# A two-block transformer kernel: first weights and tokens loaded in smaller pieces, and one sum of the second feed-forward made ahead of its gate

## What is computed

```python
def first_block(x, ...):
    h = x + mixer_block(rmsnorm(x, norm_mix_gain), w_in, ...)
    h = h + square(relu(rmsnorm(h, norm_mlp_gain) @ w_ff1)) @ w_ff2
    return rmsnorm(h, norm_final_gain)

def second_block(x, ...):
    ...
    u = rms_norm(h, pre_ffn_gain)
    gate_up = u @ w_ffn_in                       # 1024 -> 2 x 2816
    f = (silu(gate_up[..., :D_FF_2]) * gate_up[..., D_FF_2:]) @ w_ffn_out
    return h + rms_norm(f, post_ffn_gain)
```

## Time and profile before

| | |
|---|---|
| median of 3 runs | 929.07 us (928.72 to 931.43) |
| the profiled execution | 927.26 us; its span 925.5 us |
| granted TensorE clock, mean over the span | 0.999 of full |
| TensorE busy | 906.6 us, 98% of the span |
| VectorE busy | 629.2 us, 68% |
| ScalarE busy | 454.7 us, 49% |
| moved by DMA | 148.91 MB, mean 161 GB/s |

### The profile page before, as it was taken

How to read it: one execution, slowest core, us unless ns; L and a number is a source line. 1 busy time by engine, 2 the same in 40 slices (tenths; PEclk the granted TensorE clock), 3 DMA queues, 4 the chain that set the end, 5 groups by cost and what they waited for, 6 DMA issues and landing times.

```text
span 925.5 us, 13962 instructions
## 1 busy us (share of the span) xinstructions
PE 906.6 (98%) x5276; PEld 771.6 (83%) x5276; DVE 629.2 (68%) x1022; ACT 454.7 (49%) x764; POOL 43.5 (5%) x81
## 2 busy tenths in 40 slices
PE   8999999999999999989999999999999999999997
PEld 5888999998888888867776788888999778888885
DVE  5867676666876666676763777777766776666665
ACT  5646534444644444445334555666644644444443
POOL 0000010000100000010000000023310100000000
PEclk9999999999999999999999999999999999999999
DMA  9853333554655555323333222332355255555531
GB/s 347 304 203 137 137 138 137 184 181 163 224 191 194 197 193 181 136 91 137 137 136 137 91 92 92 97 132 92 105 221 206 107 187 207 196 182 181 181 136 46
DMA packets 21921, 148.91 MB, mean 161 GB/s; under 512 B 2400, under 2 KB 3168, under 8 KB 4336
## 3 DMA queue, kind: packets, MB, share of 16 engines
q1 hardware_dynamic: 20704, 145.29, 44.6%
q10 hardware_dynamic: 1168, 2.95, 0.9%
HBM read 147.18 MB, written 1.05 MB: 160 GB/s over the span
## 4 chain that ended last, share of the span: by engine, by line
PE 92%; DVE 3%; ACT 2%; issue 1%; DMA 1%; POOL 0%; SPq 0%; DVEq 0%; ACTq 0%; POOLq 0%
PE ps L432 20%; PE ps L433 19%; PE ps L434 19%; PE ps L547 14%; PE ps L548 7%; PE ps L1421 2%; PE ps L1375 1%; DVE wlo L1511 1%; PE ps L1393 1%; ACT whi L606 1%; PE ps L441 1%; PE ps L1380 1%; PE ps L444 1%; DMA raw<-weights 1%; PE ps L1111 1%
## 5 line engine op out<-in xcount | busy, mean ns | idle before, releaser
L1511 DVE TENSOR_TENSOR wlo<-raw,whi 128x2048 fp32r<-128x2048 f32 x134 | 306.8, 2290 | 152.4 <-ACT whi L606 152.0
L606 ACT ACTIVATE whi<-raw 128x2048 fp32r<-128x2048 f32 x134 | 256.3, 1914 | 184.6 <-PE ps L434 107.3
L547 PE MATMUL ps<-xT,whi 128*128 128x512 f32 x608 | 213.9, 396 | 2.6 <-DVE u_sum L2116 1.9
L548 PE MATMUL ps<-xT,wlo 128*128 128x256 f32 x608 | 169.9, 279 | 0.0
L547 PEld LDWEIGHTS ps<-xT,whi 128*128 128x128 f32 x608 | 114.1, 188 | 30.0 <-DVE wlo L1511 2.2
L432 PE MATMUL ps<-whi,xT 128*128 128x512 f32 (+1 forms) x336 | 133.3, 397 | 3.6 <-DVE wlo L1772 1.9
L434 PE MATMUL ps<-whi,xT 128*128 128x512 f32 (+1 forms) x336 | 129.6, 386 | 0.0
L433 PE MATMUL ps<-wlo,xT 128*128 128x512 f32 (+1 forms) x336 | 129.4, 385 | 0.0
L548 PEld LDWEIGHTS ps<-xT,wlo 128*128 128x128 f32 x608 | 114.6, 189 | 0.7
L432 PEld LDWEIGHTS ps<-whi,xT 128*128 128x128 f32 x336 | 63.1, 188 | 21.8 <-issue 4.3
L432 PE MATMUL ps<-xT,whi 128*128 128x256 f32 x256 | 74.7, 292 | 0.0
(11 more groups left out here) (328 smaller groups left out, 1458.2 us busy)
## 6 DMA issues: line engine op xcount, KB each, us to landing
raw<-weights SPq DMA_DIRECT2D x135, 1024.0 KB, 4.8
cst<-consts SPq DMA_DIRECT2D x1, 1595.0 KB, 13.4
raw<-weights SPq DMA_DIRECT2D x2, 512.0 KB, 6.6
gain_rows<-gain_rows ACTq DMA_DIRECT2D x1, 1024.0 KB, 8.1
y<-h ACTq DMA_DIRECT2D x4, 256.0 KB, 2.3
h<-x_tiles SPq DMA_DIRECT2D x1, 512.0 KB, 7.9
gain_row<-gain_rows ACTq DMA_DIRECT2D x1, 512.0 KB, 3.8
h<-x_tiles ACTq DMA_DIRECT2D x1, 256.0 KB, 3.0
```

The lines of the kernel that those rows point to most:

```text
L547: pe.matmul(ps[:, bank0 + j, :], vh[:, k, j * P:(j + 1) * P], xT[:, :, k, :], start=k == 0, stop=False)
L548: m = pe.matmul(ps[:, bank0 + j, 0:TOK], vl[:, k, j * P:(j + 1) * P], xT_h[:, k, :], start=False, stop=k == KC - 1)
L606: act.activation(whi[s][:], raw[s][:], ACT.Copy).then_inc(split_hi, 1)
L1511: dve.tensor_tensor(wlo[s][:], raw[s][:], whi[s][:], ALU.subtract).then_inc(split_lo, 1)
```

## The change

At the start, blobs 0 and 1 come in five loads, listed in `FIRST` as (blob, first chunk, end chunk), and the tokens in four loads of 256 columns. They are issued in the order of use. ScalarE's and VectorE's conversions and TensorE's multiplications go by the same five parts. The two squares move: the first between the last parts, the second behind the last part. TensorE's warming matmuls after the first pair of transposes are now two of 512 columns, and the second pair of transposes stands behind the first part's matmuls. In the second feed-forward the function `up_product` is split in two, `up_sum` and `up_product`. In the loop and in the last step the order of the instructions stays what it was; in step 1 ScalarE's `up_low` now stands ahead of `gate_sigmoid` and VectorE's sum ahead of `gate_product`, and `up_product` ahead of the conversion of blob F2 + 4.

```diff
+FIRST = ((0, 0, 1), (0, 1, 2), (0, 2, 4), (1, 0, 2), (1, 2, 4))
+def first_made(i):
+    n, _, end = FIRST[i]
+    return n + 1 if end == 4 else i + 1 - n
...
@@ SyncE
-            sp.dma_start(h[:, :, TOK:BANK], x[:, :, TOK:BANK]).then_inc(x_in[1], 16)
-            sp.dma_start(raw[0][:, 0:BLOB // 2], w[0][:, 0:BLOB // 2]).then_inc(first_in, 16)
-            sp.dma_start(raw[0][:, BLOB // 2:BLOB], w[0][:, BLOB // 2:BLOB]).then_inc(raw_in[0], 16)
-            sp.dma_start(h[:, :, BANK:D], x[:, :, BANK:D]).then_inc(x_in[2], 16)
-            for n in range(1, 3):
-                load(n, w[n], None)
+            load_first(0)
+            load_first(1)
+            load_tokens(1)
+            load_first(2)
+            load_tokens(2)
+            load_first(3)
+            load_tokens(3)
+            load_first(4)
+            load(2, w[2], None)
@@ ScalarE
+            def first_part(i):
+                n, k, end = FIRST[i]
+                act.wait_ge(first_in[i], 16)
+                act.activation(whi[n][:, k * BANK:end * BANK], raw[n][:, k * BANK:end * BANK],
+                               ACT.Copy).then_inc(split_hi if end == 4 else first_hi, 1)
             to_pieces(0, "norm_mix", (0, 1))
-            act.wait_ge(first_in, 16)
-            act.activation(whi[0][:, 0:BLOB // 2], raw[0][:, 0:BLOB // 2], ACT.Copy).then_inc(first_hi, 1)
+            first_part(0)
+            first_part(1)
             to_pieces(0, "norm_mix", (2, 3))
-            act.wait_ge(raw_in[0], 16)
-            act.activation(whi[0][:, BLOB // 2:BLOB], raw[0][:, BLOB // 2:BLOB], ACT.Copy).then_inc(split_hi, 1)
+            first_part(2)
             to_pieces(0, "norm_mix", (4, 5))
-            act.wait_ge(raw_in[1], 16)
-            act.activation(whi[1][:, 0:BLOB // 2], raw[1][:, 0:BLOB // 2], ACT.Copy).then_inc(first_hi, 1)
+            first_part(3)
+            square(0)
             to_pieces(0, "norm_mix", (6, 7))
-            act.activation(whi[1][:, BLOB // 2:BLOB], raw[1][:, BLOB // 2:BLOB], ACT.Copy).then_inc(split_hi, 1)
-            for t in range(NT):
-                square(t)
+            first_part(4)
+            square(1)
             hi(2)
...
             gate_low(F2 + 1)
             hi(F2 + 3)
+            up_low(F2 + 2)
             gate_sigmoid(1)
             hi(F2 + 4)
-            up_low(F2 + 2)
             hidden2_hi(1)
@@ TensorE
             pieces(0, (0, 1))
-            keep_warm(1, 1, warm, TOK)
-            pieces(0, (2, 3))
-            keep_warm(1, 1, warm)
-            keep_warm(1, 1, warm, TOK)
+            keep_warm(2, 1, warm)
+            for i, (n, k, end) in enumerate(FIRST):
+                pe.wait_ge(split_lo if end == 4 else first_lo, first_made(i))
+                multiply_tokens(pe, n, 4 * n, 4, BANK, 0, n == 0, n == 1, xT_h, xT_l, 0, ks=range(k, end))
+                if i < 3:
+                    pieces(0, (2 * i + 2, 2 * i + 3))
+            for n in range(2, MIX1):
-            for n in range(MIX1):
-                if n < 2:
-                    for part in range(2):
-                        pe.wait_ge(split_lo if part else first_lo, n + 1)
-                        multiply_tokens(pe, n, 4 * n, 4, BANK, 0, n == 0, n == 1, xT_h, xT_l, 0, part)
-                        if n == 0:
-                            pieces(0, (4 + 2 * part, 5 + 2 * part))
-                    continue
@@ VectorE
             to_pieces(0, "norm_mix", (0, 1))
-            lo_part(0, 0)
+            first_part(0)
+            first_part(1)
             to_pieces(0, "norm_mix", (2, 3))
-            lo_part(0, 1)
+            first_part(2)
             to_pieces(0, "norm_mix", (4, 5))
-            lo_part(1, 0)
+            first_part(3)
             to_pieces(0, "norm_mix", (6, 7))
-            lo_part(1, 1)
             dve.wait_ge(x_in[2], 16)
-            for t in range(NT):
-                square(t)
+            dve.wait_ge(x_in[3], 16)
+            square(0)
+            first_part(4)
+            square(1)
             lo(2)
...
             gate_norm(1)
+            up_sum(1)
             gate_product(1)
+            up_product(1)
             lo(F2 + 4)
-            up_product(1)
             hidden2_lo(1)
```

More of the change, by code:

```diff
@@ L281, in build @@
         blob_used = sem("blob_used")
-        x_in = [sem("x_in0"), sem("x_in1"), sem("x_in2")]
+        x_in = [sem(f"x_in{i}") for i in range(4)]
         early_in = sem("early_in")
         const_in = sem("const_in")
-        first_in = sem("first_in")
+        first_in = [sem(f"first_in{i}") for i in range(len(FIRST))]
         first_hi = sem("first_hi")
@@ L454, in multiply_tokens @@
             wd = min(width, BANK)
-            for k in range(nk) if part is None else range(part * nk // 2, (part + 1) * nk // 2):
+            if ks is None:
+                ks = range(nk) if part is None else range(part * nk // 2, (part + 1) * nk // 2)
+            for k in ks:
                 if chunk_wait is not None:
@@ L469, in multiply_tokens @@
                                      last and k == nk - 1)
-            if part != 0:
+            if part != 0 and nk - 1 in ks:
                 m.then_inc(blob_used, 1)
@@ L575, in _, with load_tokens, load_first @@
             sp.dma_start(cst[:, 0:EARLY], consts[:, 0:EARLY]).then_inc(early_in, 16)
-            sp.dma_start(h[:, :, TOK:BANK], x[:, :, TOK:BANK]).then_inc(x_in[1], 16)
-            sp.dma_start(raw[0][:, 0:BLOB // 2], w[0][:, 0:BLOB // 2]).then_inc(first_in, 16)
-            sp.dma_start(raw[0][:, BLOB // 2:BLOB], w[0][:, BLOB // 2:BLOB]).then_inc(raw_in[0], 16)
-            sp.dma_start(h[:, :, BANK:D], x[:, :, BANK:D]).then_inc(x_in[2], 16)
-            for n in range(1, 3):
-                load(n, w[n], None)
+            def load_tokens(q):
+                sp.dma_start(h[:, :, q * TOK:(q + 1) * TOK], x[:, :, q * TOK:(q + 1) * TOK]).then_inc(x_in[q], 16)
+            def load_first(i):
+                n, k, end = FIRST[i]
+                sp.dma_start(raw[n][:, k * BANK:end * BANK], w[n][:, k * BANK:end * BANK]).then_inc(first_in[i], 16)
+            load_first(0)
[7 more added lines that the diff above has]
+            load(2, w[2], None)
             sp.dma_start(cst[:, EARLY:NCONST], consts[:, EARLY:NCONST]).then_inc(const_in, 16)
@@ L1767, in _, with first_part @@
             dve.memset(va[:], 0.0).then_inc(init_ok, 1)
-            def lo_part(n, part):
-                a, b = part * BLOB // 2, (part + 1) * BLOB // 2
-                dve.wait_ge(split_hi if part else first_hi, n + 1)
+            def first_part(i):
+                n, k, end = FIRST[i]
+                a, b = k * BANK, end * BANK
+                dve.wait_ge(split_hi if end == 4 else first_hi, first_made(i))
                 dve.tensor_tensor(wlo[n][:, a:b], raw[n][:, a:b], whi[n][:, a:b],
-                                  ALU.subtract).then_inc(split_lo if part else first_lo, 1)
+                                  ALU.subtract).then_inc(split_lo if end == 4 else first_lo, 1)
             dve.wait_ge(early_in, 16)
             to_pieces(0, "norm_mix", (0, 1))
-            lo_part(0, 0)
+            first_part(0)
+            first_part(1)
             to_pieces(0, "norm_mix", (2, 3))
-            lo_part(0, 1)
+            first_part(2)
             to_pieces(0, "norm_mix", (4, 5))
-            lo_part(1, 0)
+            first_part(3)
             to_pieces(0, "norm_mix", (6, 7))
-            lo_part(1, 1)
             dve.wait_ge(x_in[2], 16)
-            for t in range(NT):
-                square(t)
+            dve.wait_ge(x_in[3], 16)
+            square(0)
+            first_part(4)
+            square(1)
             lo(2)
@@ L2111, in gate_product, with up_sum, up_product @@
                 dve.tensor_tensor(g_act[:], g_sum[:], g_act[:], ALU.mult).then_inc(g_one, 1)
-            def up_product(made):
+            def up_sum(made):
                 dve.wait_ge(ul_ok, made)
                 dve.tensor_tensor(u_sum[:], main_half(1), u_low[:], ALU.add).then_inc(usum_ok, 1)
+            def up_product(made):
                 dve.wait_ge(g_one, made)
@@ L2138, in _ @@
                 gate_product(i + 2)
+                up_sum(i + 2)
                 up_product(i + 2)
@@ L2145, in _ @@
             gate_product(STEP2)
+            up_sum(STEP2)
             up_product(STEP2)
```

7 lines of the change are left out of this document (4 added, 3 removed).

## The result

| | before | after |
|---|---|---|
| median, 9 runs each | 929.10 us (928.72 to 932.11) | 924.63 us (924.14 to 927.29) |
| ratio | | 0.9947, 95% interval 0.9934 to 0.9960 |
| profiled execution | 927.26 us, span 925.5 | 924.49 us, span 922.6 |

The change made the kernel faster by 0.53%: 4.5 us (interval 3.7 to 6.1) where 3.1 were forecast, and a median 0.2 us under the range (924.8 to 929.0). But the two profiled executions differ by only 2.8 us, which is about the forecast. The question is thus not only where the time came from, but why the medians show more than the traces.

The account below looks back on a forecast made before the run. TensorE, busy 98% of the span, was taken as the bound. The feed-forward's 2.03 us plus the start's 1.05 gave 3.1 us: profiled 927.26 to 924.2, and, with the median 1.8 above, 929.07 to 926.0 (range 924.8 to 929.0).

Parts of the forecast that it names:

- What bounds the kernel: Whole kernel: TensorE, busy 98% of the span; it gets shorter only where TensorE waits or its work starts late.
- the path from P to blob 2: Start: from P, where the second pair of transposes starts, TensorE reaches blob 2 at P + 14.01; before, blob 2 started at 24.48.
- The new waits: Start, TensorE: 1.6 us ahead of part 2 and 0.9 us ahead of part 4.
- The first part's landing: Start: the first 256 KB of weights land at L, and the first matmul follows at L + 1.43; gain 7.55 − L.
- L = 6.5: Start: assumed landing of the first weights, giving a first matmul at 7.93 and blob 2 at 23.43.
- TensorE waits for nothing: From blob 2 to the first turn, near 400 us: each us by which blob 2 starts earlier comes off the end.
- The later loads cost nothing: Start, loads after the first part: blob 2 lands at most near 16.9, needed at 19.1, so the price is nothing.
- The feed-forward part: Second feed-forward: without the wait for `u_sum`, TensorE starts F2 + 3 at 748.43 instead of 750.46, 2.03 us.
- the start's 1.05: Start: blob 2 at 23.43 instead of 24.48, a gain of 1.05 us (−0.5 to 1.5).
- Rival 5: Start: TensorE falls to its lower clock level at the new waits, up to 934.8 us; chance 0.10.
- Rivals 3 and 4: Start: smaller transfers each cost 2.6 us, 931.5 (0.06). Second feed-forward: the wait only changes its name, 928.0 (0.05).
- rival 2: Start: the first weights land late, at 8.06; the start loses 0.5 us, total gain 1.5, 927.5 us; chance 0.13.

Follow-up runs that it names:

- the variant: Changed kernel with both squares behind part 4 on ScalarE and VectorE, as before the change: 925.41 us (ratio 0.9960).
- start_only: Changed kernel with step 1 of the second feed-forward in its old order, so only the start part of the change: 927.59 us (0.9980).
- after_allwarm: Changed kernel plus warming matmuls in the turn between the blocks and ahead of the second feed-forward: 925.14 us in 5 executions (0.9953).
- before_turnwarm: Kernel before plus warming matmuls only in the turn between the blocks and ahead of the second feed-forward: 927.67 us (0.9977).
- ff_only: Kernel before with only the feed-forward part: in step 1 up_low and the sum moved ahead, old start: 926.12 us (0.9962).
- ff_only_2: Repeat of ff_only, the kernel before with only the feed-forward part of the change: 926.37 us (0.9966).
- after_cold: Changed kernel without the two warming matmuls of 512 columns between the first transposes and the first product: 926.05 us (0.9962).
- after_third: Changed kernel, unchanged, timed and profiled a third time: 925.18 us (0.9967 against the kernel before).
- before_again: Kernel before, unchanged, timed against itself and profiled again: 930.04 us (1.0008); profiled execution 931.24 us.

## Why the prediction missed, step by step

- *What bounds the kernel; the path from P to blob 2.* Right. P + 14.01 was forecast; 13.98 measured, and 14.61 for the variant (14.6). The new waits came within 0.2 us of their forecasts.
- *The first part's landing.* Better than forecast: the first product stood at 7.42, the lower bound given (7.5), since the load had landed when ScalarE and VectorE were done with the first pair (conversions from 5.92 and 6.69 with no wait). L = 6.5 was leaned on a single trace, in which 256 KB of tokens in this place took 5.6 us; in the eight traces with the old order they took 3.3 to 5.6, and in the ten with the new order the two first parts of weights 4.0 to 4.5. But the other side was overlooked: the tokens that are issued from ScalarE's queue land later, after 3.1 to 4.3 us instead of 3.0 to 3.4. That they now share the DMA engines with weights is the likely reason; no run has the order of the loads alone. The first transposes started at 4.17 in seven of the eight profiles with the old start (4.23 in the eighth), and between 4.17 and 5.22 in the ten with the new one, five of them waiting for the tokens' DMA (0.17 to 0.84 us).
- *From blob 2 on "TensorE waits for nothing", so that each us comes off the end "unless something later gives it back".* The exception was what happened. The absence of a wait in the trace of before said only that the spread of the norm's factor was ready in time, not by how much. It was ready at 29.93 with TensorE coming at 30.34, a slack of 0.4 us. With blob 3's load landing 0.5 us earlier than before in this pair of traces, 0.8 us could pass; the rest was given back as a wait: 0.58 us in the profile, 1.10 in `start_only`, 1.41 in `after_allwarm`. The load does not land earlier as a rule (its conversion starts between 22.29 and 23.85 in the ten traces with the new order, 22.34 and 23.61 in the seven with the old where the row stands by itself), and in `before_turnwarm` TensorE waited 0.29 us for the factor with the old order too. "The later loads cost nothing" looked at blob 2 and not at blob 3, whose load holds VectorE's list.
- *The feed-forward part, 2.03 us.* Right, and it passed through whole: the row of waiting is gone and nothing is late next. By executions at full clock `ff_only` and `ff_only_2` have 924.92 against 927.49, 2.6 us; the traces give 2.0 to 2.4, the rest is not explained.
- *The sum.* 3.1 us against 2.8 in the profiles and 2.7 at full clock. That the start's 1.05 came near the 0.80 measured is luck: the landing was taken 0.5 us too late and the give-back behind blob 2 at nothing, 0.8 us.
- *The step that failed: carrying the sum from the profiled execution to the median.* The 1.8 us by which the median of before stood above its profiled execution were taken as a constant, a term for which no reason was given. They were the cost of the lower clock level at idle places, which the profiled execution by chance met nowhere: with these places filled the same kernel has its median at 927.27. Behind the change the term was 0.1 us (924.63 against 924.49). That puts the forecast 1.7 us too high; the sum, 0.3 us too large, took some of it back, and 1.4 us of miss are left. Over all 27 executions it is 0.7 us. The medians of the two repetitions, 925.44 and 925.18, lie inside the range; by how little or much a median of nine misses is in part chance.
- *Rival 5*, the clock, was the right mechanism in the wrong kernel. It was priced for the new waits of 1.6 and 0.9 us, behind which the clock fell in none of the ten traces (in `after_cold` it was low from the first product on), instead of for the kernel before, with up to 3.2 us idle ahead of its first product. Rivals 3 and 4 did not happen; rival 2 named late weights, which did not happen, but its outcome, a start that gains nothing, did in `after_third`, by late tokens.

What stays open: why the changed kernel meets the lower level so much less. It removes two of the idle places (ahead of the first product, the wait for `u_sum`) and leaves two. Were all four alike and independent in before, 23% of executions at full clock (26 of 112) would mean a chance of 0.31 for each place, and 48% at full clock with two places left; after has 21 of 27. And they are not alike: the traces show falls mostly at the two places that stay, and none at the wait for `u_sum`. At 0.999 or more stand 5 of 12 executions of `start_only`, but only 4 of 19 of `ff_only`, about the share of before; at 0.995 or less 3 of 12 and 1 of 19, against 39 of 112. These counts are small and point both ways. So removing two places explains the direction and not the size. Filling either place alone did not give a difference outside the measurement, and filling the two that the change leaves did (2.4 us). Whether a stretch ahead of an idle place also decides if the clock falls there, no run here separates.

## What to carry to other kernels

A wait that is absent from a trace has a slack, and it must be read before a gain upstream is passed through: here, with a slack of 0.4 us, 1.58 us became 0.80. Compare the profiled execution with the median and with its granted clock before summing against it; where the median is 0.2% above, look for the idle places of TensorE and price them, for a change that removes idle time can gain both the time and the clock. One trace on each side is one draw: over all traces the start gave 0.4 us, not 0.8. Cheap matmuls in known waits turned a scatter of 3.6 us into one of 1.5 (0.3 for seven of nine executions), at no cost in a clean execution.

## What the runs showed of the hardware

- TensorE fell to half its clock after idle times as short as the 1 to 3 us of these waits, in some executions and not in others of the same kernel: after 3.20 us idle in one profile, not after 3.03 us in another (`ff_only`). The fall at the start of `before_again` cost 1.56 us, about the distance between the classes of the table (927.49 to 929.11).
- The Trainium skill, TensorE: Matmul & The Clock Gate, section Why this matters for your kernels, advises no idle gaps over about 3 us between bursts of matmuls. The traces agree for the gap of 3.20 us and not for that of 3.03, and at 417 us the clock fell though no single wait there was over 1.3 us; between the waits stood 16 transposes and some 15 narrow matmuls (listed as 128*48 and 128*16).
- Matmuls at the lower level stepped by 0.43 us and at the upper by 0.23, for 512 columns.
- The first warming matmuls, from 1.45 us, run slowly in every profile, and the granted clock is listed as 1.00 there. It is also listed as 1.00 between 5 and 15 us in `after_cold`, whose products step by 0.43 us until about 13. In the first stretch the durations are the evidence, not that column.
- Two loads of 256 KB of weights, issued second and third by SyncE, landed in 4.0 to 4.5 us (medians of ten traces); 256 KB of tokens in the second place took 3.3 to 5.6 in the eight traces with the old order.
